# A two-layer decoder trunk on one core: the host lays out input, constants and result channel-major, TensorE makes the first scale, and the mask takes one VectorE and one ScalarE operation

## The reference, cut to what matters

```
c_act = silu(c)
for l in range(2):
    sh1, sc1, g1, sh2, sc2, g2 = split(c_act @ w_ada[l] + b_ada[l], 6)     # each of 1024 channels
    h = rms_norm(x, norm1_g[l]) * (1.0 + sc1) + sh1
    u, cq, ckv, kr, gate_a, gate_b = split(h @ w_in[l])
    y_a = s5_mixer(u, ssm parameters of l) @ w_a_out[l]
    y_b = mla_mixer(cq, ckv, kr, positions, cos, sin, ...) @ w_b_out[l]    # masked by positions[k] <= positions[q]
    x = x + g1 * ((sigmoid(gate_a) * y_a + sigmoid(gate_b) * y_b) @ w_out[l])
    h = rms_norm(x, norm2_g[l]) * (1.0 + sc2) + sh2
    x = x + g2 * ((silu(h @ w_gate[l]) * (h @ w_up[l])) @ w_down[l])
return rms_norm(x, final_g)
```

## Time and profile before

| | |
|---|---|
| median of three runs | 3465.75 us (3465.4 to 3468.68) |
| the profiled execution's own time | 3466.75 us |
| its span, first to last instruction | 3464.9 us |
| mean granted TensorE clock | 0.960 of full speed |
| busy: PE, DVE, ACT, POOL | 3226.9, 1667.2, 1013.7, 974.6 us |

### The profile page before, as it was taken

The page is one execution under the profiler, slowest core; times in us unless marked ns, Lnnn a source line. Parts: engine busy times, 40 slices in busy tenths (PEclk is TensorE's granted clock), DMA queues, the critical chain, the costliest instruction groups (busy, mean ns, idle before and its releaser), DMA issues.

```text
span 3464.9 us, 42628 instructions
## 1 busy us (share of the span) xinstructions
PE 3226.9 (93%) x15640; PEld 2704.1 (78%) x15640; DVE 1667.2 (48%) x1859; ACT 1013.7 (29%) x1387; POOL 974.6 (28%) x543
## 2 busy tenths in 40 slices
PE   2799989999889999999989998999988999999997
PEld 1788879987668887888788887898766778877875
DVE  7778628765452222222378772787455132222223
ACT  1323237762121111111132333677212211111112
POOL 2265322222222222221236541132232212212212
PEclk6899989999989999999999998999998999999998
DMA  5355410013531111111135451011353111111111
GB/s 162 142 163 155 129 51 15 23 47 127 164 75 54 48 43 48 48 42 48 43 123 165 136 155 58 11 26 35 121 170 86 43 49 48 42 48 48 43 48 55
DMA packets 280231, 272.13 MB, mean 79 GB/s; under 512 B 68574, under 2 KB 234636, under 8 KB 278796
## 3 DMA queue, kind: packets, MB, share of 16 engines
q1 hardware_dynamic: 273452, 228.21, 22.0%
q10 hardware_dynamic: 6624, 41.95, 3.3%
HBM read 226.00 MB, written 44.11 MB: 78 GB/s over the span
## 4 chain that ended last, share of the span: by engine, by line
PE 86%; DVE 5%; issue 4%; ACT 2%; DMA 1%; POOL 1%; SPq 1%; DVEq 0%; ACTq 0%; POOLq 0%
PE ps L512 22%; PE ps L515 21%; PE ps L514 21%; PE ps L1268 3%; PE ps L1252 2%; PE ps L1257 2%; PE ps L1256 2%; PE ps L1289 2%; PE ps L1288 2%; DVE ada_acc L1790 2%; PE ps L1054 1%; PE ps L1055 1%; PE ps L1056 1%; DMA ada_raw<-in_w_ada 1%; PE ps L1087 1%
## 5 line engine op out<-in xcount | busy, mean ns | idle before, releaser
L497 POOL TENSOR_TENSOR wlo<-raw,whi 128x1024 fp32r<-128x1024 f32 (+3 forms) x290 | 544.6, 1886 | 2057.7 <-ACT whi L489 2056.8
L489 ACT ACTIVATE whi<-raw 128x1024 fp32r<-128x1024 f32 (+3 forms) x290 | 242.7, 859 | 1825.4 <-PE ps L515 1754.6
L512 PE MATMUL ps<-h_hi,whi 128*128 128x512 f32 x2048 | 655.8, 401 | 24.3 <-DVE h_lo L1886 10.1
L514 PE MATMUL ps<-h_lo,whi 128*128 128x512 f32 x2048 | 646.9, 397 | 0.0
L515 PE MATMUL ps<-h_hi,wlo 128*128 128x512 f32 x2048 | 646.6, 397 | 0.0
L512 PEld LDWEIGHTS ps<-h_hi,whi 128*128 128x128 f32 x2048 | 383.5, 190 | 111.5 <-POOL wlo L497 11.1
L514 PEld LDWEIGHTS ps<-h_lo,whi 128*128 128x128 f32 x2048 | 389.0, 190 | 92.8
L515 PEld LDWEIGHTS ps<-h_hi,wlo 128*128 128x128 f32 x2048 | 388.0, 189 | 91.9
L2228 DVE TENSOR_TENSOR silu<-silu,ps 128x1024 f32<-128x1024 f32 x44 | 53.8, 1222 | 830.4 <-PE ps L515 809.3
L2240 DVE SCALAR_TENSOR_TENSOR x_sb<-ps,mod,x_sb 128x1024 f32<-128x1024 f32 x176 | 223.9, 1281 | 216.9 <-PE ps L515 216.9
L512 PE MATMUL ps<-hid_hi,whi 128*128 128x512 f32 x704 | 223.3, 398 | 6.5 <-DVE x_sb L2240 6.5
(11 more groups left out here) (290 smaller groups left out, 4955.9 us busy)
## 6 DMA issues: line engine op xcount, KB each, us to landing
ada_raw<-in_w_ada SPq DMA_DIRECT2D x112, 512.0 KB, 4.2
raw<-in_w_in SPq DMA_DIRECT2D x92, 256.0 KB, 3.7
raw<-in_w_gate SPq DMA_DIRECT2D x88, 256.0 KB, 3.2
raw<-in_w_up SPq DMA_DIRECT2D x88, 256.0 KB, 3.3
raw<-in_w_down SPq DMA_DIRECT2D x88, 256.0 KB, 2.9
gate_scratch<-gst ACTq DMA_DIRECT2D x32, 512.0 KB, 3.4
gl<-gate_scratch SPq DMA_DIRECT2D x32, 512.0 KB, 4.2
xs_scratch<-x_sb ACTq DMA_DIRECT2D x2, 4096.0 KB, 12.4
```

Source lines behind the costliest of these rows:

```text
L489: last = act.activation(dst(whi[:, s, :]), src(raw[:, s, :]), ACT.Copy)
L497: last = pool.tensor_tensor(dst(wlo[:, s, :]), src(raw[:, s, :]), dst(whi[:, s, :].bitcast(F32)), ALU.subtract)
L512: pe.matmul(o, w_h, x_h, start=first, stop=False)
L514: pe.matmul(o, w_h, x_l, start=False, stop=False)
```

## The change

The host now hands over x transposed (channels by tokens), takes the result in the same form, and packs constants: `row_consts` (all biases and gains as columns, for `cols`), `pos_q` (positions as a 128 by 8 table), and `state_space`, one row of 2176 floats for each of 128 partitions and layer. So 4 constant loads take the place of 19, one load of 1.1 MB that of the 14 parameter loads, x goes straight to `x_sb`, and the transposes and copies at the start, at the head of each layer and at the end are gone. `fin` is stored tile by tile as VectorE makes it. The first scale is made by PE from the rows of `w_ada` (its tiles go to a pair of buffers of their own, `first_raw`), so VectorE has eight rounds of `ada_product` in place of 16. A mask tile is one VectorE operation and one Relu of ScalarE with a scale of 2^93. The order on VectorE changes: the tables come ahead of `a1`.

```diff
-CONSTS = 19
+CONSTS = 4
@@ SP, start
-            for t in range(TT):
-                sp.dma_start(x_in[:, t, :], x[0, t * P:(t + 1) * P, :]).then_inc(x_in_loaded.sem, 16)
-            for m in range(2):
-                for k in range(KT):
-                    n = m * KT + k
-                    load_ada(0, slice(m * D, (m + 1) * D), k, 0, n - 1 if n >= 2 else None)
-                if m == 0:
-                    s5_parameters(0)
+                sp.dma_start(s5p[:, :], state_space[l]).then_inc(s5_loaded.sem, 16)
+
+            for k in range(KT):
+                sp.dma_start(x_sb[:, k, :], x[k * P:(k + 1) * P, :]).then_inc(x_in_loaded.sem, 16)
+            for k in range(KT):
+                s = k % 2
+                if k >= 2:
+                    sp.wait_ge(first_mm.sem, k - 1)
+                sp.dma_start(first_raw[:, s, :], w_ada[0][k * P:(k + 1) * P, D:2 * D]).then_inc(first_loaded[2 + s].sem, 16)
+                if k >= 2:
+                    sp.wait_ge(ada_used.sem, k - 1)
+                sp.dma_start(ada_raw[:, s, :], w_ada[0][k * P:(k + 1) * P, 0:D]).then_inc(first_loaded[s].sem, 16)
+            s5_parameters(0)
@@ SP, end
-            for t in range(TT):
-                sp.wait_ge(fin_ev.sem, t + 1)
-                sp.dma_start(out[0, t * P:(t + 1) * P, :], o_row[:, t % 2, :]).then_inc(out_done[t % 2].sem, 16)
+            for k in range(KT):
+                sp.wait_ge(fin_t.sem, k + 1)
+                sp.dma_start(out[k * P:(k + 1) * P, :], fin[:, k, :]).then_inc(out_done.sem, 16)
@@ PE, start (the transposes of prow and x_in are gone)
+            pe.wait_ge(act_const.sem, 1)
             for k in range(KT):
+                pe.wait_ge(first_loaded[2 + k % 2].sem, 16 * (k // 2 + 1))
+                for n in range(KT):
+                    last = pe.matmul(ps[:, 0, n:n + 1], first_raw[:, k % 2, n * P:(n + 1) * P], c_act[:, k:k + 1],
+                                     start=(k == 0 and n == 0), stop=(k == KT - 1), skip_group_check=True)
+                last.then_inc(first_mm.sem, 1)
...
+            pe.wait_ge(ada_used.sem, KT)
+            mod_products()
@@ ACT, start
+            act.wait_ge(x_in_loaded.sem, 16 * KT)
             for k in range(KT):
                 squares(0, 0, k)
+                if k == 0:
+                    act.wait_ge(angles_ready.sem, 1)
+                    act.activation(sin_t[:, :], ang[:, :], ACT.Sin).then_inc(act_const.sem, 1)
+                    act.activation(ang_k[:, :], half[:, :], ACT.Sin).then_inc(act_const.sem, 1)
+                act.wait_ge(mask_sum.sem, k + 1)
+                act.activation(mask[:, k, :], mask_t[:, k % 2, :], ACT.Relu, bias=lo_bias[:, k:k + 1], scale=MASK_UNIT)\
+                    .then_inc(mask_step.sem, 1)
@@ DVE, start
-            for m in range(2):
-                for k in range(KT):
-                    ada_product(-1, 4 * KT + m * KT + k, k)
-                    if m == 0 and k % 2:
-                        dve.wait_ge(xt_mm.sem, k + 1)
-                        dve.tensor_copy(x_sb[:, k, :], pair(4)).then_inc(xt_dve.sem, 1)
-                    if k % 2 == 0:
-                        ... three operations for one mask tile ...
+            for k in range(KT):
+                if k >= 2:
+                    dve.wait_ge(mask_step.sem, k - 1)
+                dve.scalar_tensor_tensor(mask_t[:, k % 2, :], pos_f[:, :], hi_bias[:, k:k + 1], pos_lo[:, :],
+                                         ALU.subtract, ALU.add).then_inc(mask_sum.sem, 1)
+                ada_product(-1, 5 * KT + k, k)
...
+            dve.wait_ge(mask_step.sem, KT)
             dve.sem_inc(tables_ready.sem, 1)
+            dve.wait_ge(first_mm.sem, KT)
+            dve.tensor_tensor(mod[:, 1, :], ps[:, 0, 0:KT], cols[:, 0, ROW_B_ADA + KT:ROW_B_ADA + 2 * KT], ALU.add)\
+                .then_inc(mod_ready.sem, 1)
+            dve.wait_ge(mod_ready.sem, 1)
+            dve.scalar_tensor_tensor(a1[:, :], mod[:, 1, :], 1.0, cols[:, 0, ROW_N1:ROW_N1 + KT], ALU.add, ALU.mult)\
+                .then_inc(a1_ready.sem, 1)
+            modulation(-1, 5, 0, mod[:, 0, :], cols[:, 0, ROW_B_ADA:ROW_B_ADA + KT])
```

More of the change, by code:

```diff
@@ L72, in rope_rows, with column_rows, state_space_rows, both @@
     return t
-def trunk(nc, x, c, positions, w_ada, b_ada, norm1_g, w_in, ssm_a_re, ssm_a_im, ssm_log_dt, ssm_b_re,
-          ssm_b_im, ssm_c_re, ssm_c_im, ssm_d, w_glu, b_glu, w_a_out, q_norm_g, w_uq, kv_norm_g, w_uk,
-          w_uv, w_b_out, w_out, norm2_g, w_gate, w_up, w_down, final_g, rope_const, out):
+def column_rows(c, b_ada, norm1_g, norm2_g, b_glu, q_norm_g, kv_norm_g, final_g):
+    rows = np.zeros((P, b_ada.shape[0], ROWS), np.float32)
+    for first, v in ((ROW_B_ADA, b_ada), (ROW_N1, norm1_g), (ROW_N2, norm2_g), (ROW_BGLU, b_glu), (ROW_QN, q_norm_g),
+                     (ROW_KVN, kv_norm_g), (ROW_C, c), (ROW_FG, final_g[None])):
+        n = v.shape[1] // P
+        rows[:, :, first:first + n] = v.reshape(v.shape[0], n, P).transpose(2, 0, 1)
+    return rows
+def state_space_rows(a_re, a_im, log_dt, b_re, b_im, c_re, c_im, d):
+    depth, groups = a_re.shape[:2]
+    def both(re, im):
+        return np.concatenate([re, im], axis=1).reshape(depth, P, -1)
+    b_rows = [v.transpose(0, 2, 1, 3) for v in (b_re, b_im)]
+    c_rows = [v.transpose(0, 3, 1, 2) for v in (c_re, c_im)]
+    a_rows = [v.transpose(0, 2, 1) for v in (a_re, a_im)]
+    d_rows = np.tile(d.reshape(depth, groups, SSM_GROUP).transpose(0, 2, 1), (1, P // SSM_GROUP, 1))
+    dt_rows = np.broadcast_to(log_dt[:, None, :], (depth, P, groups))
+    return np.ascontiguousarray(np.concatenate(
+        [both(*b_rows), both(*b_rows[::-1]), both(*c_rows), both(*c_rows[::-1]), both(a_rows[0], a_rows[0]),
+         both(a_rows[1], a_rows[1]), d_rows, dt_rows], axis=2))
+def trunk(nc, x, positions, pos_q, row_consts, state_space, rope_const, w_ada, w_in, w_glu, w_a_out, w_uq, w_uk, w_uv,
+          w_b_out, w_out, w_gate, w_up, w_down, out):
     DEPTH, D, _ = w_ada.shape
@@ L1425, in _ @@
             norm_scale(DEPTH, 0)
-            for t in range(TT):
-                if t == 0:
-                    pe.wait_ge(fin_t.sem, KT)
-                if t >= 2:
-                    pe.wait_ge(fin_ev.sem, t - 1)
-                b = 2 * (t % 2)
-                for k in range(KT):
-                    last = pe.transpose(ps[:, b + k // 4, (k % 4) * P:(k % 4 + 1) * P], fin[:, k, t * P:(t + 1) * P],
-                                        ident[:, 0:P])
-                last.then_inc(fin_mm.sem, 1)
         @block.scalar
@@ L1441, in copy @@
                 return act.activation(dst, src, ACT.Copy)
-            act.wait_ge(dve_const.sem, DVE_CONSTS + 1)
+            act.wait_ge(dve_const.sem, DVE_CONSTS)
+            act.wait_ge(const_loaded.sem, 16 * CONSTS)
             act.activation(c_act[:, :], cols[:, 0, ROW_C:ROW_C + KT], ACT.Silu).then_inc(act_const.sem, 1)
-            for k in range(0, KT, 2):
-                act.wait_ge(xt_mm.sem, k + 1)
-                copy(x_sb[:, k, :], pair(2)).then_inc(xt_act.sem, 1)
-            act.wait_ge(angles_ready.sem, 1)
-            act.activation(sin_t[:, :], ang[:, :], ACT.Sin).then_inc(act_const.sem, 1)
-            act.activation(ang_k[:, :], half[:, :], ACT.Sin).then_inc(act_const.sem, 1)
             def squares(l, ahead, k):
@@ L1755, in _ @@
             norm(DEPTH, 0, None)
-            for t in range(TT):
-                act.wait_ge(fin_mm.sem, t + 1)
-                if t >= 2:
-                    act.wait_ge(out_done[t % 2].sem, 16 * (t // 2))
-                copy(o_row[:, t % 2, :], pair(2 * (t % 2))).then_inc(fin_ev.sem, 1)
         @block.vector
```

189 lines of the change are left out of this document (56 added, 133 removed).

## The result

The changed kernel takes 3356.07 us (median of four runs, 3354.7 to 3357.16). The kernel before took 3466.64 us beside it (3465.4 to 3468.68). The ratio is 0.968, with a 95% interval from 0.9664 to 0.9697: 110.6 us less.

What follows compares the result with a forecast made beforehand. The prediction took DVE to bound the start and PE the body of large matmuls. Gains of 43 us at the start and 15 at the end made 58 us, so 3408 us from a median of 3465.75, range 3393 to 3421.

Steps and rivals of the forecast that it cites:

- DVE almost without a break from 13.01 to 90.6: Start of the kernel before: the chain of waits was read as running through DVE between these times in us.
- Constants at 5.9 us, VectorE at 6.3: Start: constants landed at 5.9 us, between bounds 4.8 and 6.7; DVE begins its angles at 6.3, not 13.01.
- The loop, 34.3 us to 52.7: DVE's mask and product rounds: 20.3 us of operations plus 14 for seven POOL meetings, ending at 52.7 us.
- The rival that the buffers set it: Loop at the start: load buffers, not the DVE-POOL lock, set its length; ends at 40 to 48 us; chance 0.20.
- PE's groups in 3.6 us, the last done at 49: PE in the loop: eight groups of one-column products, 3.6 us each, done at 49 us, hidden behind DVE.
- rival 2: Loop at the start: SP's alternate waits make loads serial, 8.2 us a round; total 3438 us; chance 0.08.
- From the loop to rstd, 11.4 us, and to the first large matmul, 8.9: Behind the loop: tables, two lengthened splits and small operations until rstd at 64.1 us; first large matmul at 73.0.
- The end, 15 us, the stores' rate sets it, last landing 12 to 13 us behind the first tile: End of the kernel: fin stores at 1.31 us a tile set the rate, saving 15 us; bounds 12.2 and 15.8.
- Rival 3: End of the kernel: stores of channel rows from fin queue up and the end gains nothing; 3423 us; chance 0.04.
- The head of the second layer at 0: Second layer's start: removing 11 transposes and four copies gains 0, since the root waits for ACT's table load.
- Rival 4, the clock: Body: earlier start brings more time at half clock, making the kernel slower, 3473 us with 130 us more; chance 0.02.
- The step that failed: Body between first and last large matmul: taken as unchanged within 0.2%, so only start and end gain, 58 us.

Runs made afterwards that it cites:

- e9: Changed kernel with six of the seven additions of squares at the start on 8 of 1024 columns; 3350.61 us, ratio 0.9667 to the kernel before.
- e10: Changed kernel with the first store of the result held back until all eight fin tiles are made; 3364.08 us, ratio 0.9705 to the kernel before.
- e1: Changed kernel with 1152 unused bytes ahead of the activations, so they lie at their old addresses; 3408.61 us, ratio 0.9832 to the kernel before.

## Why the prediction was wrong, point by point

- **DVE almost without a break from 13.01 to 90.6.** Misread. In that stretch the chain leaves VectorE three times for loads, for 26.7 us in all: from 42.58 to 59.89 us it runs through SP, which issues the 14 parameter loads and only then the next tile of `ada_raw`, and two more tiles are waited for later:

```profile
55.63 4.24 DMA ada_raw<-in_w_ada
...
74.66 4.47 DMA ada_raw<-in_w_ada
...
80.53 4.73 DMA ada_raw<-in_w_ada
```

  The forecast did not need this reading, since it adds up the new loop from its own operations. But a good part of the start's gain is these waits, and not VectorE's work.
- **Constants at 5.9 us, VectorE at 6.3.** Late by 1.1 and 2.4 us. The positions took 4.90 us from issue to landing, above the upper of the two bounds (4.58). The last to land was the broadcast table, which neither bound was measured on. The table load of 1.28 us between constants and `c_act` was not in the sum.
- **Preparation of 12.1 us.** Held: 8.70 to 20.76.
- **The loop, 34.3 us to 52.7.** 33.3 us, to 54.1. Seven meetings with POOL as said, at 2.1 us each in place of 2.0; the operations themselves took 1.6 us less than the 20.3, since they follow each other every 1.20 us (39.37, 40.57, 41.77). The rival that the buffers set it was not the case, but near: e9 puts it some 5 us behind. The Trainium skill, SBUF — State Buffer, section SBUF: two separate sides, says that the lock lasts for a whole instruction. The trace agrees, since VectorE goes on only when the addition ends (25.01 to 28.38 around 27.29). The 3413 us of the estimate with 2.7 us for each meeting did not come. An addition that meets no VectorE operation takes 2.34 us (at 3330.44 in the chain of waits), so the 2.7 held POOL's own waits, and a meeting costs VectorE 2.1 us of those 2.34.
- **PE's groups in 3.6 us, the last done at 49.** They took 3.57 us, the last done at 50.9. The forecast's lower bound took half of 3.59 us for them at full clock. That was wrong: the granted clock was 1.00 from 18.7 to 50.9 us, and a group took what it took before at 0.50. SP's two waits in turn did not make the loads serial: rival 2 did not happen.
- **From the loop to rstd, 11.4 us, and to the first large matmul, 8.9.** 11.4 and 9.0. The two `wlo` splits lengthened two operations of the tables, as said. But these two (L1801 at 55.26 us, 2.88 us long, and L1802 at 58.17, 2.72) read one tensor from SBUF and not two; with POOL idle, in e9, they take 0.69 and 0.81. In the kernel before, mask operations with one such input (L1847 at 61.04, 2.83 us in the timeline, against 0.75 at 74.48) were lengthened as well. So the condition of two SBUF inputs, as the prediction puts it, is too narrow.
- **The end, 15 us, the stores' rate sets it, last landing 12 to 13 us behind the first tile.** 15.2 us and 12.1; e10 shows that it is the rate. Rival 3 did not happen.
- **The head of the second layer at 0.** e1 has the same body within 1.4 us, so it holds.
- **Rival 4, the clock.** It did not happen: 0.969 over the span, and 0.97 in the body as before.
- **The step that failed** is the one ahead of all these: "Everything between is a body of large matmuls. So the change is worth what it moves the first large matmul ... forward ... and what it cuts behind the last fin tile", and with it "the body ... as long as before within 0.2%". It was 1.6% shorter, 52.8 us. The sentence in front, "Nothing in the change touches the large matmuls", was true of the instructions and false of their operands' addresses. At the old place (e1) the changed kernel takes 3408.61 us, and 3408 was the forecast. So the miss is this step, but for errors of about 1 us at the start that partly cancel. No rival had it, and the range, made from start and end alone, could not hold it.

The kernel before held the evidence that a gain was possible there only in part: its large matmuls at 233 ns. Nothing in its trace shows the same matmuls at a second pace. The addresses were to be had from the sizes in the diff.

**What stays open.** Why the remainder matters. The runs show that it acts on PE's pace and that it needs both the weights' and the activations' place. No other engine takes part in it, by the window above. That the weight load and the read of the moving operand get in each other's way is the nearest reading, but it is argued and not shown. The weight and activation tiles of these matmuls all lie at multiples of 256 bytes from their block's start, so one number describes the case. A remainder of 0 alone is not enough for 227 ns: the score matmuls, whose operands both lie at multiples of 1024 from the block's start, run at 230.5.

## What to carry to other kernels

When an edit changes the size of any tile in SBUF, write down the distance, modulo 256 bytes, between the tiles that TensorE reads as weights and as moving operand, before and after, and look at the starts of consecutive matmuls for their pace. A packed or removed constant can move everything behind it. For a fair test of the edit itself, run it with the old placement too, and for a cheap gain, try the placement alone: here it was worth 1.6%. When a stretch is bound by VectorE operations of float32 tiles in SBUF, count the GpSimd additions in it, and at 1024 columns put 2.1 us on each.

## What the runs showed of the hardware that was not expected

- The pace of a stream of float32 matmuls of 512 columns, each with its own weights, depends on the distance between weights and activations in a partition: 227.1 ns on average at a remainder of 0 by 256 bytes, 229.0 at 64, 232.6 to 232.7 at 128, and 233.3 at 32, 192 and 224. The slow pace holds while no other engine and no DMA works. Over the kernel that is 3354 to 3356 us at 0, 3375 at 64, 3409 at 128, and 3415 to 3416 at 32, 192 and 224. Shifting both by 224 bytes changes nothing (3355.68).
- A VectorE operation with two SBUF inputs and a GpSimd addition of 1024 columns alternate at 3.3 us a pair, where VectorE alone takes 1.27. A VectorE operation with one SBUF input is lengthened too, from 0.69 to 2.88 us.
- Eight one-column float32 products with their weights (16 instructions) take 3.57 us at a granted clock of 1.00 and 3.59 us at 0.50.
- ScalarE's table load started at 0.74 us, ahead of the constants, when one wait stood before the operation that needs it, and at 7.11 us, behind them, when two did.
- 4.19 MB of result in eight stores take 12.1 to 12.2 us from the first issue, both when the stores are spaced by VectorE (issues over 8.70 us) and when they are issued at once.
